# Down projections inside the MLP loops: one 128-row weight block by 1024 columns per unit, summed over a whole turn in four PSUM banks

## The chip, the cores and the metric

The kernel runs on one core of a Trainium2 chip. The metric is the device time of one execution in microseconds, as the median of several runs. Three runs of the kernel before gave 2069.18, 2069.45 and 2069.55 us.

## The reference, cut to what matters

Two layers of an encoder act on x, which has 256 rows of 2048 float32 values. Each layer adds the output of an attention stage and then that of an MLP with 8192 hidden columns. The change touches only the MLP's second product.

```python
for l in range(DEPTH):                      # DEPTH = 2
    ...                                     # attention stage, x = x + mixed @ w_out[l]
    h2 = rmsnorm(x, norm2_g[l])             # x: (256, 2048)
    x = x + jnp.square(jax.nn.relu(h2 @ w_up[l])) @ w_down[l]
    # w_up[l]: (2048, 8192), w_down[l]: (8192, 2048)
```

## The kernel before

**Units.** All large products are cut into units of weights. A unit is a tile of 128 partitions by 2 by 512 float32 values (512 KB) in one of the eight slots of `raw_ring`. In the MLP a unit of w_up holds two row blocks of 128 rows by 512 columns, and so does a unit of w_down. SyncE loads it (line 389), up to eight units ahead. ScalarE (`split_hi`, line 715) rounds it to `w_hi`, and VectorE (`split_lo`, line 894) subtracts to get the rest, `w_lo`. The activations are held as two such halves too. Both `w_hi` and `w_lo` have four slots (`AHEAD` = 4), taken in turn, so that unit s + 4 goes where unit s was. `split_hi` of unit s + 4 therefore waits in `unit_done` until TensorE has finished unit s, and `split_lo` of it waits in `hi_ready` for `split_hi`.

**Order.** Each engine runs a program written out in steps s, one per unit. In step s TensorE multiplies unit s, while ScalarE and VectorE first split unit s + 4 and then do the other work of the step. A layer has its attention steps, then 32 up units, then three turns (`LOOPS`) of 32 down units and 32 up units, then 32 down units. Each turn consumes the hidden columns (2048 of them, `ht`, hi and lo) of the up units before it.

**Down units before** (`rows_unit`, lines 482 to 504). A turn has eight chunks `c` of four units `k`. A chunk is 512 columns of x, summed over 1024 of the hidden columns; the sums of the two row halves of x (`r` = 0, 1) fill two PSUM banks. A unit is eight matmuls with `w_hi` (line 496, two row blocks, two halves of x, two halves of `ht`) and four with `w_lo` (line 500). Chunks take the bank pairs 4, 5 and 2, 3 in turn, and a chunk waits in `evicted` for the chunk before last. After a chunk's last unit VectorE adds both banks, scaled by `rstd`, to x (line 1164), in the step's program behind `split_lo(pl, s + AHEAD)` (line 1146).

**Up units** (`up_unit`, lines 506 to 521). A chunk of eight units fills four banks, 0 to 3 or 4 to 7 in turn (`up_banks`), by 8 matmuls of 512 columns (line 516) and 8 of 256 (line 519) in each unit. The first chunk of a turn's up units takes banks 4 to 7.

Of the kernel before, what the change touches and what calls it, by code (L numbers as in the profile page):

```python
# [24 lines left out]
ALU = mybir.AluOpType  # L25
# [3 lines left out]
P = 128  # L29
D = 2048  # L30
# [36 lines left out]

CHUNKS = NPROJ + 4 + 48  # L70
EVICTIONS = [(CHUNKS - 1) // 2, CHUNKS // 2]
LOOP_EVICTIONS = 6


SUMMED_UNITS = list(range(55, 83, 2))
# [85 lines left out]
def vector_splits(n):  # L161

    return n - sum(u < n for u in SUMMED_UNITS)
# [7 lines left out]
def encoder(nc, x_in, norm1_g, w_in, a_qnorm_g, a_knorm_g, a_rel_bias, b_qnorm_g, b_knorm_g, b_sinks, c_qnorm_g,  # L171
            c_knorm_g, c_lambda_q1, c_lambda_k1, c_lambda_q2, c_lambda_k2, c_subln_g, w_out, norm2_g, w_up, w_down,
            consts, out):
    with ExitStack() as ctx:
# [3 lines left out]
        def sem(name):  # L178
            return ctx.enter_context(nc.semaphore(name))
# [110 lines left out]
        mid_loaded = sem("mid_loaded")  # L290
        stored = sem("stored")
        row0_done, row0_out = sem("row0_done"), sem("row0_out")

        H_CHUNKS = 16

# [23 lines left out]
        def mlp_steps(first, kinds):  # L319


            s, n = first, {UP0: 13, LOOP0: 17, DOWN3: 17 + 36}[first]
            for kind in kinds:
                if kind == "up":
                    for q in range(4):
                        for k in range(UPC):
                            yield s, "up", q // 2, q, k, n
                            s += 1
                        n += 1
                else:  # L330
                    for c in range(8):
                        for k in range(4):
                            yield s, "down", c // 4, c, k, n
                            s += 1
                        n += 1

        def layer_steps(eng, l, do_mix, do_mlp):

            pl = Place(l)
            for s in range(UP0):  # L340
                do_mix(pl, s)
            for st in mlp_steps(UP0, ["up"]):
                do_mlp(pl, *st)
            for i in range(LOOPS):
                for st in mlp_steps(LOOP0, ["down", "up"]):
                    do_mlp(Place(l, i), *st)
            for st in mlp_steps(DOWN3, ["down"]):
                do_mlp(pl, *st)
# [11 lines left out]
        def late_chunk(s, part, c, k, lag):  # L360

            if part == "up":
                if k == lag and c > 0:
                    return c - 1, (c - 1) + (0 if s < LOOP0 else 4)
                return None
            if c == 0 and k == lag:

                return 3, 3 if s < DOWN3 else 3 + 4 * LOOPS
            return None

        def used(pl, s):
# [11 lines left out]
        def _(sp):  # L383
            def load(pl, u, w, width, offset, cols):
                if u - RAWS in SUMMED_UNITS:
                    sp.wait_ge(*lo_sum_of(pl, u - RAWS))
                else:
                    sp.wait_ge(split_done, pl.at(VECTOR_SPLITS, vector_splits(u - RAWS + 1) + RAWS, LOOP_UNITS))
                sp.dma_start(raw_ring[:, u % RAWS, :, 0:cols],
                             bass.AP(w.tensor, offset, [[width, P], [P * width, 2], [1, cols]])).then_inc(raw_loaded[u % RAWS], 16)  # L390
# [31 lines left out]
            def load_up(pl, u, c, k):  # L422

                i = 0 if pl.i is None else pl.i
                col = (c + (0 if u < LOOP0 else 4)) * CW + i * (4 * CW)
                load(pl, u, w_up, D_FF, pl.l * (D * D_FF) + k * 2 * P * D_FF + col, CW)

            def load_down(pl, u, c, k, past=False):
                i = 0 if pl.i is None else pl.i
                row = (c // 4 + (2 * LOOPS if past else 0)) * (D_FF // 8) + k * 2 * P  # L430
                load(pl, u, w_down, D, pl.l * (D_FF * D) + i * (2 * (D_FF // 8) * D) + (row * D + (c % 4) * CW), CW)

            def mlp(pl, s, part, buf, c, k, n):

                u = s + FIRST_LOADS
                if part == "up":
                    n = c * UPC + k + FIRST_LOADS
                    if n < 4 * UPC:
                        load_up(pl, u, n // UPC, n % UPC)
                    elif s < LOOP0:  # L440
                        load_down(pl, u, 0, n - 4 * UPC)
                    else:
                        load_down(pl, u, 8, n - 4 * UPC)
                else:
                    n = c * 4 + k + FIRST_LOADS
                    if n < 32:
                        load_down(pl, u, n // 4, n % 4, s >= DOWN3)
                    elif s < DOWN3:
                        load_up(pl, u, 0, n - 32)
                    elif pl.l < DEPTH - 1:  # L450
                        load_proj(pl, u, pl.l + 1)

# [22 lines left out]
        def _(pe):  # L475
# [30 lines left out]
            def up_unit(pl, u, k, chunk):  # L506

                slot, p, bank = u % AHEAD, chunk % 2, up_banks(chunk)
                if k == 0:
                    pe.wait_ge(evicted[p], pl.evictions(chunk))  # L510
                pe.wait_ge(hi_ready, pl.unit(u + 1))
                tiles = [(2 * k + j, f, slot, j) for j in range(2) for f in range(4)]
                for kt, f, w, j in tiles:
                    both = xt_both[:, kt, :, :].rearrange("p h q -> p (h q)")

                    pe.matmul(bank[:, f, :], w_hi[:, w, j, f * P:(f + 1) * P], both, start=kt == 0, stop=False, skip_group_check=True)  # L516
                unit_is_split(pl, u)
                for kt, f, w, j in tiles:
                    mm = pe.matmul(bank[:, f, 0:SEQ], w_lo[:, w, j, f * P:(f + 1) * P], xt[0][:, kt, :], start=False,  # L519
                                   stop=kt == KT - 1, skip_group_check=True)  # L520
                mm.then_inc(unit_done, 1)

            def warm(n):

# [144 lines left out]
            def mlp(pl, s, part, buf, c, k, n):  # L669
                if part == "up":  # L670
                    if s < LOOP0 and c == 0:
                        pe.wait_ge(panel_done, pl.at(PANELS, PANELS_BEFORE + FIRST_X2 + k + 1))
                    if s == UP0:
                        pe.wait_ge(maxed, pl.at(JOBS, JOBS + 1))
                        pe.wait_ge(pt_copied, pl.at(FILLS, FILLS + 1))
                    if s == UP0 + UPC:
                        pe.wait_ge(pv_copied, pl.at(MIXES, MIXES + 1))
                        pe.wait_ge(t_free, pl.at(T_USES, T_BEFORE + T_NUMBER[OUT_LAST[3] + 4] + 1))
                    up_unit(pl, s, k, n)
                else:  # L680
                    if k == 0 and c % 4 == 0:

                        done = (4 if s >= DOWN3 else 0) + 2 * (buf + 1) + (8 if s >= DOWN3 else 0)
                        pe.wait_ge(h_done, pl.at(H_CHUNKS, done, 4))
                    rows_unit(pl, s, ht, (8 * buf + 2 * k, 8 * buf + 2 * k + 1), n, k == 0, k == 3, CW)
                if s in T_USE and used(pl, s):
                    use_t(pl, s)
# [195 lines left out]
        def _(dve):  # L883
# [257 lines left out]
            def mlp(pl, s, part, buf, c, k, n):  # L1141
# [4 lines left out]
                    split_lo(pl, s + AHEAD)  # L1146
                if s == UP0 + 2:
                    row_norm(pl, 1)
                if part == "down" and k == 3:
                    p = n % 2  # L1150
                    if c == 0:
                        dve.wait_ge(rstd_ready, pl.at(2, 2))
                    final = pl.l == DEPTH - 1 and s == UNITS - 1
                    if not final:
                        dve.wait_ge(unit_done, pl.unit(s + 1 + AHEAD))
                    dve.wait_ge(evicted[p], pl.evictions(n))
                    for r in range(RT):
                        v = x[:, r, (c % 4) * CW:(c % 4 + 1) * CW]
                        if final and r == 0:
                            dve.wait_ge(row0_done, 1)  # L1160
                        if final and r == 1:
                            last.then_inc(row0_out, 1)
                            dve.wait_ge(unit_done, pl.unit(s + 1 + AHEAD))
                        last = dve.scalar_tensor_tensor(v, acc[:, 2 * p + r, :], rstd[:, 1, r:r + 1], v, ALU.mult, ALU.add)  # L1164
                    last.then_inc(evicted[p], 1)
# [6 lines left out]
                late = late_chunk(s, part, c, k, 0)  # L1172
                if late is not None:
                    q, count = late
                    m = n - 1
                    dve.wait_ge(evicted[m % 2], pl.evictions(m) + 1)
                    dve.scalar_tensor_tensor(mlp_t[q % 2][:, :], mlp_t[q % 2][:, :], 0.0, mlp_t[q % 2][:, :], ALU.max,  # L1177
                                             ALU.mult).then_inc(relu2, 1)
# [202 lines left out]
```

## Time and profile before

| | |
|---|---|
| median of three runs | 2069.45 us (2069.18 to 2069.55) |
| span of the profiled execution, first to last instruction | 2067.1 us |
| own time of the profiled execution | not listed separately; the runs' median is 2.35 us above its span |
| TensorE busy | 2061.8 us |
| VectorE busy | 1267.3 us |
| ScalarE busy | 990.7 us |
| DMA, mean | 192 GB/s |

The profile records one execution. PE is TensorE's matmuls and PEld its weight loads, DVE is VectorE, ACT is ScalarE, POOL is GpSimd and SP is SyncE; a "q" behind a name is the engine's instruction queue. Matmul records overlap their neighbours, so the spacing of two starts, and not the duration of one, tells what a matmul costs in a row. Lines with x and a number are several instructions merged, and their duration is that of the group from its first start to its last end.

### The profile page before, as it was taken

How to read it: one execution, taken by the hardware profiler on the slowest of the kernel's cores; microseconds unless marked ns; L12 is line 12 of the kernel's file. 1: busy time of each engine (PE TensorE's matmuls, PEld its weight loads, DVE VectorE, ACT ScalarE, POOL GpSimd, SP SyncE). 2: the span in 40 equal slices, each digit the busy share in tenths (PEclk: the TensorE clock that was granted, in tenths of full speed). 3: DMA queues.
4: the chain of work that ended last, by engine and by line, in shares of the span. 5: the costliest groups of instructions: out<-in, count | busy, mean ns of one | idle time of the engine just before them, and what ended most of it. 6: DMA issues, size and time to landing. Idle time of an engine off the chain costs nothing.

```text
span 2067.1 us, 26774 instructions
## 1 busy us (share of the span) xinstructions
PE 2061.8 (100%) x10762; PEld 1733.5 (84%) x10762; DVE 1267.3 (61%) x1646; ACT 990.7 (48%) x1328; POOL 191.7 (9%) x196
## 2 busy tenths in 40 slices
PE   9999999999999999999999999999999999999999
PEld 7887788888888888888888877888888888888887
DVE  7767566655565556556677775665655655665664
ACT  6557644443443444344455586444434434434442
POOL 6253100000000000001023531000000000000000
PEclk9999999999999999999999999999999999999999
DMA  9477866666666666666665689666666666666663
GB/s 301 136 229 194 225 184 184 191 191 192 189 192 194 187 190 193 193 185 193 183 178 148 205 203 242 176 183 190 192 192 190 192 194 187 191 193 192 186 193 122
DMA packets 207451, 396.64 MB, mean 192 GB/s; under 512 B 13674, under 2 KB 22352, under 8 KB 207328
## 3 DMA queue, kind: packets, MB, share of 16 engines
q1 hardware_dynamic: 202640, 379.52, 61.9%
q0 software_dynamic: 4512, 15.33, 4.0%
q8 instruction: 85, 1.39, 0.3%
q14 instruction: 38, 0.31, 0.0%
q10 hardware_dynamic: 176, 0.09, 0.0%
HBM read 377.95 MB, written 2.12 MB: 184 GB/s over the span
## 4 chain that ended last, share of the span: by engine, by line
PE 99%; DMA 0%; SPq 0%; DVE 0%; issue 0%
PE psum L496 40%; PE psum L516 23%; PE psum L500 20%; PE psum L519 12%; PE psum L531 1%; PE psum L603 1%; PE psum L582 0%; PE psum L628 0%; PE psum L590 0%; PE psum L588 0%; DMA x<-in_x_dram 0%; PE psum L638 0%; PE psum L619 0%; PE psum L620 0%; PE psum L618 0%; PE psum L640 0%
## 5 line engine op out<-in xcount | busy, mean ns | idle before, releaser
L894 DVE TENSOR_TENSOR w_lo<-raw_ring,w_hi 128x1024 fp32r<-128x1024 f32 (+1 forms) x692 | 850.9, 1231 | 680.8 <-ACT w_hi L715 679.4
L715 ACT CAST w_hi<-raw_ring 128x1024 fp32r<-128x1024 f32 (+1 forms) x720 | 749.7, 1042 | 995.3 <-PE psum L500 604.1
L516 PE MATMUL psum<-xt,w_hi 128*128 128x512 f32 x2048 | 512.9, 392 | 0.0
L496 PE MATMUL psum<-w_hi,ht_hi 128*128 128x512 f32 x1280 | 501.8, 392 | 0.0
L496 PE MATMUL psum<-w_hi,ht_lo 128*128 128x512 f32 x1280 | 498.6, 390 | 0.0
L516 PEld LDWEIGHTS psum<-xt,w_hi 128*128 128x128 f32 x2048 | 368.8, 189 | 66.3
L500 PE MATMUL psum<-w_lo,ht_hi 128*128 128x512 f32 x1280 | 342.5, 389 | 0.0
L519 PEld LDWEIGHTS psum<-xt,w_lo 128*128 128x128 f32 x2048 | 279.4, 190 | 19.9
L519 PE MATMUL psum<-xt,w_lo 128*128 128x256 f32 x2048 | 285.6, 282 | 0.0
L500 PEld LDWEIGHTS psum<-w_lo,ht_hi 128*128 128x128 f32 x1280 | 240.3, 188 | 50.3
L496 PEld LDWEIGHTS psum<-w_hi,ht_hi 128*128 128x128 f32 x1280 | 240.4, 188 | 49.6 <-issue 1.0
L496 PE MATMUL psum<-w_hi,xt 128*128 128x512 f32 (+1 forms) x1152 | 281.5, 386 | 0.0
L496 PEld LDWEIGHTS psum<-w_hi,ht_lo 128*128 128x128 f32 x1280 | 240.5, 188 | 48.8
L496 PEld LDWEIGHTS psum<-w_hi,xt 128*128 128x128 f32 x1152 | 202.4, 188 | 40.9 <-issue 2.7
L500 PE MATMUL psum<-w_lo,xt 128*128 128x512 f32 (+1 forms) x576 | 147.8, 378 | 0.0
L500 PEld LDWEIGHTS psum<-w_lo,xt 128*128 128x128 f32 x576 | 104.8, 188 | 21.1 <-DMA w_lo<-raw_ring 0.3
L1164 DVE SCALAR_TENSOR_TENSOR x<-psum,rstd,x 128x512 f32<-128x512 f32 x128 | 89.9, 743 | 6.4 <-PE psum L500 6.4
L1278 POOL TENSOR_TENSOR rope_c<-const,gains 128x64 f32<-128x64 f32 x16 | 9.6, 597 | 706.9 <-DVE head_sq L1177 701.1
L1028 DVE COPY probs_t<-psum 128x256 f32<-128x256 f32 (+1 forms) x56 | 26.8, 479 | 39.8 <-PE psum L603 39.8
L730 ACT CAST xt<-panel 128x512 fp32r<-128x512 f32 x32 | 19.9, 620 | 53.1 <-DVE panel L919 52.9
L1286 POOL TENSOR_TENSOR small<-small 128x16 f32<-128x16 f32 (+2 forms) x16 | 40.8, 2549 | 1.3
L1340 POOL DMA_DIRECT2D w_lo<-raw_ring x28 | 24.6, 897 | 130.1 <-ACT w_lo L717 130.1
(144 smaller groups left out, 968.2 us busy)
## 6 DMA issues: line engine op xcount, KB each, us to landing
raw_ring<-in_w_up_dram SPq DMA_DIRECT2D x256, 512.0 KB, 3.7
raw_ring<-in_w_down_dram SPq DMA_DIRECT2D x256, 512.0 KB, 3.7
raw_ring<-in_w_in_dram SPq DMA_DIRECT2D x128, 512.0 KB, 4.7
raw_ring<-in_w_out_dram SPq DMA_DIRECT2D x64, 512.0 KB, 4.8
w_lo<-raw_ring POOLq DMA_DIRECT2D x28, 512.0 KB, 5.8
raw_ring<-in_w_in_dram SPq DMA_DIRECT2D x16, 256.0 KB, 2.8
x<-in_x_dram SPq DMA_DIRECT2D x8, 256.0 KB, 7.5
out_dram<-x SPq DMA_DIRECT2D x3, 512.0 KB, 2.7
```

The source lines that it names most:

```text
L496: pe.matmul(bank[r][:, 0:cols], t[:, kt, r * P:(r + 1) * P], w_hi[:, slot, j, 0:cols], start=first and j == 0 and n == 0, stop=False, skip ...
L500: mm = pe.matmul(bank[r][:, 0:cols], src[0][:, kt, r * P:(r + 1) * P], w_lo[:, slot, j, 0:cols], start=False, stop=last and j == 1, skip_g ...
L516: pe.matmul(bank[:, f, :], w_hi[:, w, j, f * P:(f + 1) * P], both, start=kt == 0, stop=False, skip_group_check=True)
L519: mm = pe.matmul(bank[:, f, 0:SEQ], w_lo[:, w, j, f * P:(f + 1) * P], xt[0][:, kt, :], start=False, stop=kt == KT - 1, skip_group_check=True)
L531: mm = pe.transpose(bank[:, n * P:(n + 1) * P], b, ident)
L603: mm = pe.transpose(ps_p[:, n * P:(n + 1) * P], probs[:, j % 4, n * P:(n + 1) * P], ident)
L715: act.copy(w_hi[:, u % AHEAD, :, 0:cols], raw_ring[:, u % RAWS, :, 0:cols]).then_inc(hi_ready, 1)
L894: dve.tensor_tensor(w_lo[:, u % AHEAD, :, 0:cols], raw_ring[:, u % RAWS, :, 0:cols], w_hi[:, u % AHEAD, :, 0:cols].bitcast(F32), ALU.subtr ...
L1028: dve.tensor_copy(probs_t[:, f % 3, cols], ps_p[:, cols]).then_inc(pt_copied, 1)
L1164: last = dve.scalar_tensor_tensor(v, acc[:, 2 * p + r, :], rstd[:, 1, r:r + 1], v, ALU.mult, ALU.add)
L1286: return pool.tensor_tensor(dst, v, minus_half[:, 0:n], ALU.pow)
L1340: pool.dma_start(w_lo[:, u % AHEAD, :, :], raw_ring[:, u % RAWS, :, :], accum_op=ALU.add).then_inc(lo_sum_of(pl, u)[0], 16)
```

## The change

In the three turns of both layers, the 32 down units are now `pair` steps. A unit is one row block of 128 rows by 1024 columns, loaded in rows of 4 KB (before: two row blocks by 512 columns, in rows of 2 KB). Sixteen units `m` run over all 16 row blocks of the turn, for the left 1024 columns of x (`d` = 0) and then for the right ones (`d` = 1). The sums for two halves of x and two halves of the columns lie in banks 4 to 7, and are added to x after m = 15, one bank at a time. Both values of `d` use the same four banks, and so does the first chunk of up units that follows. TensorE therefore waits in `pair_out` for bank n before it starts the new sum there. In the last unit of a sum, TensorE finishes one bank after the other and signals `pair_done` for the first three. The 32 down units at the end of a layer stay as they were.

The diff, cut to its core:

```diff
-CHUNKS = NPROJ + 4 + 48
+CHUNKS = NPROJ + 4 + 4 + 4 * LOOPS + 8
 EVICTIONS = [(CHUNKS - 1) // 2, CHUNKS // 2]
-LOOP_EVICTIONS = 6
+LOOP_EVICTIONS = 2
+
+
+PAIR_UNITS = 32
+BLOCKS = 2 * UPC
+PAIR_OUTS = 4
...
+                if kind == "pair":
+                    for d in range(2):
+                        for m in range(BLOCKS):
+                            yield s, "pair", None, d, m, None
+                            s += 1
...
+        def pair_at(pl, u):
+
+            w = u - LOOP0 + LOOP_UNITS * (pl.i or 0)
+            if 0 <= w < LOOPS * LOOP_UNITS and w % LOOP_UNITS < PAIR_UNITS:
+                return w // LOOP_UNITS, w % PAIR_UNITS // BLOCKS, w % BLOCKS
...
+            def load_pair(pl, u, turn, d, m):
+
+                sp.wait_ge(split_done, pl.at(VECTOR_SPLITS, vector_splits(u - RAWS + 1) + RAWS, LOOP_UNITS))
+                sp.dma_start(raw_ring[:, u % RAWS, :, :].rearrange("p j n -> p (j n)"),
+                             bass.AP(w_down.tensor, pl.l * (D_FF * D) + (turn * D + m * P) * D + d * 2 * CW,
+                                     [[D, P], [1, 2 * CW]])).then_inc(raw_loaded[u % RAWS], 16)
...
+                    if kt == 0 and pl.i is not None and chunk == 17:
+                        pe.wait_ge(pair_out, pl.at(2 * LOOPS * PAIR_OUTS, PAIR_OUTS + f + 1, 2 * PAIR_OUTS))
...
+            def pair_step(pl, s, d, m):
+
+                outs = pl.at(2 * LOOPS * PAIR_OUTS, d * PAIR_OUTS, 2 * PAIR_OUTS)
+                if d == 0 and m in (0, UPC):
+                    pe.wait_ge(h_done, pl.at(H_CHUNKS, 2 + 2 * (m // UPC), 4))
+                if d == 0 and m == 0:
+                    pe.wait_ge(evicted[1], pl.evictions(17))
+                pe.wait_ge(hi_ready, pl.unit(s + 1))
+                if m == BLOCKS - 1:
+                    unit_is_split(pl, s)
+                for n in range(4):
+                    r, h = n // 2, n % 2
+                    bank = psum[:, 4 + n, :]
+                    if d == 1 and m == 0:
+                        pe.wait_ge(pair_out, outs - PAIR_OUTS + 1 + n)
+                    for j, t in enumerate(ht):
+                        pe.matmul(bank, t[:, m, r * P:(r + 1) * P], w_hi[:, s % AHEAD, h, :], start=m == 0 and j == 0,
+                                  stop=False, skip_group_check=True)
+                    if m == BLOCKS - 1:
+                        mm = pe.matmul(bank, ht[0][:, m, r * P:(r + 1) * P], w_lo[:, s % AHEAD, h, :], start=False, stop=True,
+                                       skip_group_check=True)
+                        mm.then_inc(pair_done if n < 3 else unit_done, 1)
+                if m < BLOCKS - 1:
+                    unit_is_split(pl, s)
+                    for n in range(4):
+                        r, h = n // 2, n % 2
+                        mm = pe.matmul(psum[:, 4 + n, :], ht[0][:, m, r * P:(r + 1) * P], w_lo[:, s % AHEAD, h, :], start=False,
+                                       stop=True, skip_group_check=True)
+                    mm.then_inc(unit_done, 1)
...
                     split_lo(pl, s + AHEAD)
                 if s == UP0 + 2:
                     row_norm(pl, 1)
+                if part == "pair" and k == BLOCKS - 1:
+                    if pl.i == 0 and c == 0:
+                        dve.wait_ge(rstd_ready, pl.at(2, 2))
+                    for g in range(4):
+                        r, h = g // 2, g % 2
+                        if g < 3:
+                            dve.wait_ge(pair_done, pl.at(2 * LOOPS * 3, 3 * c + g + 1, 6))
+                        else:
+                            dve.wait_ge(unit_done, pl.unit(s + 1 + AHEAD))
+                        v = x[:, r, (2 * c + h) * CW:(2 * c + h + 1) * CW]
+                        dve.scalar_tensor_tensor(v, psum[:, 4 + g, :], rstd[:, 1, r:r + 1], v, ALU.mult, ALU.add).then_inc(pair_out, 1)
```

## Rows read from the trace of the kernel before

**Rows 1.** The page's span and busy times of all engines.

```profile
span 2067.1 us, 26774 instructions
...
PE 2061.8 (100%) x10762; PEld 1733.5 (84%) x10762; DVE 1267.3 (61%) x1646; ACT 990.7 (48%) x1328; POOL 191.7 (9%) x196
```

**Rows 2.** The page's chain that ended last, by engine and by line.

```profile
PE 99%; DMA 0%; SPq 0%; DVE 0%; issue 0%
PE psum L496 40%; PE psum L516 23%; PE psum L500 20%; PE psum L519 12%; PE psum L531 1%; PE psum L603 1%; PE psum L582 0%; PE psum L628 0%; PE psum L590 0%; PE psum L588 0%; DMA x<-in_x_dram 0%; PE psum L638 0%; PE psum L619 0%; PE psum L620 0%; PE psum L618 0%; PE psum L640 0%
```

**Rows 3.** Busy times, granted clock (PEclk), DMA share and GB/s, a stretch of the first layer's loops.

```profile
core 0: us, PE busy (x) PEld busy (x) DVE busy (x) ACT busy (x) POOL busy (x), PEclk, DMA share, GB/s
...
545.00:700.00 155.00, 155.00 (x775) 131.92 (x775) 89.45 (x82) 64.84 (x63) 0.00 (x0) 1.00 0.66 191
```

**Rows 4.** TensorE in order of time, around a down unit's end.

```profile
start us, us, engine line op out<-in xcount [idle before <-releaser]
429.60 0.62 PE L500 MATMUL psum<-w_lo,ht_hi 128*128 128x512 f32 x2
430.05 0.39 PE L496 MATMUL psum<-w_hi,ht_hi 128*128 128x512 f32 x1
430.27 0.39 PE L496 MATMUL psum<-w_hi,ht_lo 128*128 128x512 f32 x1
...
431.86 1.07 PE L500 MATMUL psum<-w_lo,ht_hi 128*128 128x512 f32 x4
432.77 0.39 PE L496 MATMUL psum<-w_hi,ht_hi 128*128 128x512 f32 x1
```

**Rows 5.** TensorE in order of time, up units.

```profile
520.15 2.00 PE L516 MATMUL psum<-xt,w_hi 128*128 128x512 f32 x8
521.99 1.11 PE L519 MATMUL psum<-xt,w_lo 128*128 128x256 f32 x8
522.94 2.00 PE L516 MATMUL psum<-xt,w_hi 128*128 128x512 f32 x8
```

**Rows 6.** ScalarE in order of time, the down unit's end.

```profile
430.30 1.05 ACT L715 CAST w_hi<-raw_ring 128x1024 fp32r<-128x1024 f32 x1 [1.67 <-PE psum L500]
```

**Rows 7.** VectorE in order of time, the down unit's end.

```profile
431.38 1.23 DVE L894 TENSOR_TENSOR w_lo<-raw_ring,w_hi 128x1024 fp32r<-128x1024 f32 x1 [0.36 <-ACT w_hi L715]
432.53 1.40 DVE L1164 SCALAR_TENSOR_TENSOR x<-psum,rstd,x 128x512 f32<-128x512 f32 x2
434.11 1.23 DVE L894 TENSOR_TENSOR w_lo<-raw_ring,w_hi 128x1024 fp32r<-128x1024 f32 x1 [0.18 <-ACT w_hi L715]
```

**Rows 8.** The page's DMA issues of the down weights: count, KB each, us to landing.

```profile
raw_ring<-in_w_down_dram SPq DMA_DIRECT2D x256, 512.0 KB, 3.7
```

**Rows 9.** The page's costliest groups, additions onto x: count, busy us, mean ns, idle before.

```profile
L1164 DVE SCALAR_TENSOR_TENSOR x<-psum,rstd,x 128x512 f32<-128x512 f32 x128 | 89.9, 743 | 6.4 <-PE psum L500 6.4
```

**Rows 10.** VectorE, 8 to 10 us, a tile TensorE waits for.

```profile
8.35 1.22 DVE L894 TENSOR_TENSOR w_lo<-raw_ring,w_hi 128x1024 fp32r<-128x1024 f32 x1
```

**Rows 11.** TensorE's weight loads, 8 to 10 us.

```profile
9.62 0.53 PEld L500 LDWEIGHTS psum<-w_lo,xt 128*128 128x128 f32 x3 [0.23 <-DVE w_lo L894]
```

**Rows 12.** TensorE in order of time, the kernel's start.

```profile
1.14 1.65 PE L692 MATMUL psum<-panel 128*128 128x128 f32 x6 [1.14 <-DVE panel L1225]
...
2.96 1.54 PE L526 MATMUL psum<-const 128*128 128x128 f32 x6
4.29 0.91 PE L531 MATMUL psum<-const,x 128*128 128x128 f32 x4
5.03 1.25 PE L526 MATMUL psum<-const 128*128 128x128 f32 x10
7.05 0.66 PE L531 MATMUL psum<-const,x 128*128 128x128 f32 x4 [0.76 <-DMA x<-in_x_dram]
...
9.67 1.14 PE L500 MATMUL psum<-w_lo,xt 128*128 128x512 f32 x4
```

**Rows 13.** The warming transposes' line: count, duration in ns min/median/max.

```profile
L526 PE MATMUL psum<-const x18: 272/273/474, 3.0 to 7.7; 128*128 128x128 f32 x18
```

**Rows 14.** Busy times and granted clock (PEclk), two stretches of the start.

```profile
3.00:4.00 1.00, 1.00 (x6) 1.00 (x6) 0.19 (x1) 0.00 (x0) 0.00 (x0) 1.00 0.73 200
...
5.00:6.00 1.00, 1.00 (x11) 1.00 (x10) 0.69 (x1) 0.00 (x0) 0.00 (x0) 1.00 0.93 299
```

More of the change, by code:

```diff
@@ L292, in encoder @@
         row0_done, row0_out = sem("row0_done"), sem("row0_out")
+        pair_done, pair_out = sem("pair_done"), sem("pair_out")
         H_CHUNKS = 16
@@ L319, in mlp_steps @@
         def mlp_steps(first, kinds):
-            s, n = first, {UP0: 13, LOOP0: 17, DOWN3: 17 + 36}[first]
+            s, n = first, {UP0: 13, LOOP0: 17, DOWN3: 17 + 4 * LOOPS}[first]
             for kind in kinds:
-                if kind == "up":
+                if kind == "pair":
[3 more added lines that the diff above has]
+                            s += 1
+                elif kind == "up":
                     for q in range(4):
@@ L344, in layer_steps @@
             for i in range(LOOPS):
-                for st in mlp_steps(LOOP0, ["down", "up"]):
+                for st in mlp_steps(LOOP0, ["pair", "up"]):
                     do_mlp(Place(l, i), *st)
@@ L368, in late_chunk @@
                 return 3, 3 if s < DOWN3 else 3 + 4 * LOOPS
+            return None
+        def pair_at(pl, u):
+            w = u - LOOP0 + LOOP_UNITS * (pl.i or 0)
+            if 0 <= w < LOOPS * LOOP_UNITS and w % LOOP_UNITS < PAIR_UNITS:
+                return w // LOOP_UNITS, w % PAIR_UNITS // BLOCKS, w % BLOCKS
             return None
@@ L426, in load_up, with load_down @@
                 load(pl, u, w_up, D_FF, pl.l * (D * D_FF) + k * 2 * P * D_FF + col, CW)
[L428 to L431, printed above, removed]
+            def load_down(pl, u, c, k):
+                row = (c // 4 + 2 * LOOPS) * (D_FF // 8) + k * 2 * P
+                load(pl, u, w_down, D, pl.l * (D_FF * D) + (row * D + (c % 4) * CW), CW)
+            def load_pair(pl, u, turn, d, m):
[3 more added lines that the diff above has]
+                                     [[D, P], [1, 2 * CW]])).then_inc(raw_loaded[u % RAWS], 16)
             def mlp(pl, s, part, buf, c, k, n):
                 u = s + FIRST_LOADS
-                if part == "up":
+                if pair_at(pl, u) is not None:
+                    load_pair(pl, u, *pair_at(pl, u))
+                elif part == "pair":
+                    load_up(pl, u, 0, u - LOOP0 - PAIR_UNITS)
+                elif part == "up":
                     n = c * UPC + k + FIRST_LOADS
@@ L439, in mlp @@
                         load_up(pl, u, n // UPC, n % UPC)
-                    elif s < LOOP0:
+                    else:
                         load_down(pl, u, 0, n - 4 * UPC)
-                    else:
-                        load_down(pl, u, 8, n - 4 * UPC)
                 else:
@@ L446, in mlp @@
                     if n < 32:
-                        load_down(pl, u, n // 4, n % 4, s >= DOWN3)
-                    elif s < DOWN3:
-                        load_up(pl, u, 0, n - 32)
+                        load_down(pl, u, n // 4, n % 4)
                     elif pl.l < DEPTH - 1:
@@ L679, in mlp @@
                     up_unit(pl, s, k, n)
+                elif part == "pair":
+                    pair_step(pl, s, c, k)
                 else:
                     if k == 0 and c % 4 == 0:
-                        done = (4 if s >= DOWN3 else 0) + 2 * (buf + 1) + (8 if s >= DOWN3 else 0)
-                        pe.wait_ge(h_done, pl.at(H_CHUNKS, done, 4))
+                        pe.wait_ge(h_done, pl.at(H_CHUNKS, 4 * LOOPS + 2 * (buf + 1)))
                     rows_unit(pl, s, ht, (8 * buf + 2 * k, 8 * buf + 2 * k + 1), n, k == 0, k == 3, CW)
@@ L1148, in mlp @@
                     row_norm(pl, 1)
+                if part == "pair" and k == BLOCKS - 1:
[5 more added lines that the diff above has]
+                            dve.wait_ge(pair_done, pl.at(2 * LOOPS * 3, 3 * c + g + 1, 6))
+                        else:
+                            dve.wait_ge(unit_done, pl.unit(s + 1 + AHEAD))
+                        v = x[:, r, (2 * c + h) * CW:(2 * c + h + 1) * CW]
+                        dve.scalar_tensor_tensor(v, psum[:, 4 + g, :], rstd[:, 1, r:r + 1], v, ALU.mult, ALU.add).then_inc(pair_out, 1)
                 if part == "down" and k == 3:
@@ L1174, in mlp @@
                     q, count = late
-                    m = n - 1
+                    m = 16 if part == "pair" else n - 1
                     dve.wait_ge(evicted[m % 2], pl.evictions(m) + 1)
```

## The prediction

> **What bounds the kernel now.** I read the page's busy times first: TensorE is busy for 2061.8 of 2067.1 us, while VectorE stands at 1267.3 and ScalarE at 990.7 [rows 1]. The reader should see that an edit can only shorten this kernel by making TensorE's own stream shorter, since TensorE idles for 5.3 us in all. The chain that ended last says the same: 99% of it is TensorE, and all of it that matters is matmul lines [rows 2]. In a stretch of the loops TensorE is busy for all of 155.00 us, at a granted clock of 1.00, and the DMA engines are busy for 0.66 of it [rows 3]. So no wait ends last in the loops: there is no waiting left to take away there, only waiting to add.
>
> Then I looked at the cost of one unit. The spacing of matmul starts counts. In a down unit the eight with w_hi start at 430.05 and the four with w_lo at 431.86, so the spacing is 1.81 / 8 = 0.227 us. The next unit starts at 432.77, so a unit takes 2.72 us [rows 4]. In an up unit eight matmuls last 2.00 us from first start to last end; with 0.39 for the last one the spacing is 1.61 / 7 = 0.23 us, and the unit takes 522.94 - 520.15 = 2.79 us [rows 5].
>
> Last I looked at what happens when a unit ends, because the change makes TensorE wait there. The unit that ends at 430.22 (two matmuls from 429.60, 0.62 us long [rows 4]) frees its slot of w_hi. ScalarE's rounding of the unit four ahead starts at 430.30 and takes 1.05 us [rows 6]. Only then can VectorE's subtraction for that unit start, at 431.38, and behind it in VectorE's program stands the addition onto x, at 432.53 [rows 7]. So the addition starts 2.48 us after TensorE has begun the next unit (432.53 - 430.05). In the kernel before nobody waits for it: the next chunk uses the other pair of banks, and its own banks are wanted again only four units, or 10.9 us, later.
>
> **The change part by part.**
>
> *Matmuls.* A pair unit has 4 x 2 matmuls with w_hi and 4 with w_lo, all of 512 columns: 12, as before, from the same kinds of operand. There are 6 turns x 32 = 192 such units. Only the bank order differs. I cost this at nothing, at 0.227 us each. Bounds: the nearest rows of another loop, the up units', have 0.230 us [rows 5], which would add 2304 x 0.003 = 7 us at most. A gain isn't excluded but small, since 1 ns each is 2.3 us and the rows of two quite different orders (0.227 and 0.230) differ by 3 ns.
>
> *Loads.* 512 KB per unit as before, in half as many rows of twice the length. A load lands in 3.7 us [rows 8], and is issued about eight units (21.8 us) ahead of its use, so it could take several times as long before anyone noticed. It costs nothing and brings nothing; if that cover were gone, TensorE would wait for DMA, which it does nowhere in the loops now. SyncE's wait for each load is the same wait in split_done, so its queue isn't delayed.
>
> *Additions onto x.* Before, a turn had 8 chunks x 2 of them, now 2 x 4. That is 6 x 8 = 48 fewer, at 0.743 us each [rows 9] some 36 us of VectorE's time. VectorE has 1267 us of work in 2067 [rows 1] and TensorE waits for it nowhere in the loops, so the saving is worth nothing.
>
> *The wait in h_done for the second half of the hidden columns* comes at m = 8 instead of unit 16. The last of these tiles is made in steps 0 to 2 of the turn by both programs, five units earlier than needed. Nothing.
>
> *The new waits in pair_out.* This is what I think decides. Before m = 15 of d = 0 the four banks can't be added, and d = 1 starts in the same banks at once. The signals pair_done are given early, in the last unit itself, but VectorE can't use them: in step m = 15 its program first has split_lo of the unit four ahead, which waits for split_hi, which waits in unit_done for the end of this very unit. So the first addition starts no earlier than now, 2.48 us after TensorE would have started d = 1. TensorE's queue is in order, so everything behind that wait stands as well.
>
> Take the rows of the boundary at 430.05 as a template. The first addition runs from 432.53 to 432.53 + 0.743 = 433.27 [rows 7, 9]. From a VectorE result to TensorE's next weight load 0.05 us pass (8.35 + 1.22 = 9.57 against 9.62) [rows 10, 11], and the matmul starts 0.05 us after the load (9.67) [rows 12]. So TensorE starts at 433.37 instead of 430.05: 3.32 us late. It then needs a bank each 2 x 0.227 = 0.45 us, but two additions take 1.40 us together, so one follows another by 1.40 - 0.74 = 0.66 us [rows 7]. The additions set the pace for three more banks: bank four is started at 433.37 + 3 x 0.66 = 435.35, and its pair ends its turn at 435.80. Undisturbed it would have been 430.05 + 8 x 0.227 = 431.86. The loss between d = 0 and d = 1 is 3.94 us.
>
> After d = 1 the up units take the same banks, and there each bank gets only one matmul before the next is wanted. The fourth starts at 435.35 as well and is through at 435.58, against 430.05 + 4 x 0.23 = 430.97: a loss of 4.61 us. What is late next? Three more units are already split, and VectorE is through with its four additions about 5.0 us after the old unit's end (432.53 - 430.22 = 2.31, then 3 x 0.66 + 0.74), before TensorE ends the delayed unit, 2.72 + 3.94 = 6.7 us after it was due to start. So nothing is handed on, and the loss of each stall stands alone.
>
> Into d = 0 of a turn there is no such wait: the up chunk before it lies in banks 0 to 3, and the one before that was emptied eight units ago.
>
> There are 6 turns, with one of each: 6 x (3.94 + 4.61) = 51.3 us. Bounds from the rows: if only the first bank's wait counted, 12 x 3.32 = 40 us; if each addition, now with a signal of its own, ran its full 0.743 us and no more overlapped its neighbour, 12 x 3 x 0.09 = 3 us more, so 54 us, and with the first bound on the matmuls 61 us.
>
> **The sum.** 2067.1 + 51.3 = 2118.4 us of span. The runs' median lies 2.35 us above the profile's span, so 2120.8 us.
>
> **A rule on the clock.** At the kernel's start six transposes take 1.54 us and ten take 1.25 us a little later [rows 12]; with 0.47 and 0.27 for the last of each (the longest and the median record of that line [rows 13]) the spacings are 0.21 and 0.11 us, a factor of two, as between 1.2 and 2.4 GHz, although the granted clock reads 1.00 in both stretches [rows 14]. The slow pace was over by the group at 5.03, and a gap of 0.76 us at 7.05 did not bring it back. This case has no longer gap, so it can't say what one of 3.3 us does. The Trainium skill ("TensorE: Matmul & The Clock Gate", "Why this matters for your kernels") says that idle gaps of TensorE between bursts can put it back to 1.2 GHz; it speaks against this change, as the stalls above are such gaps. No run here shows it yet. By it the sum would be that of the second rival below; without it the 51 us stand.
>
> **The rivals.**
>
> 1. *The evictions slip under the last unit, and nothing is lost.* The code in TensorE's last unit finishes banks 0.68 us apart (3 x 0.227), an addition every 0.66 us would keep up, and bank n would be free long before d = 1 asks. This needs VectorE to reach the additions before unit m = 15 ends. Against it stands the order of [rows 4, 6, 7]: rounding, subtraction, addition, each behind the unit's end, and the new additions stand at the same place of the program. If it held, the time would be 2069.4, and any nanosecond that the longer rows or fewer additions take off the matmuls' spacing would come on top: at 2 ns, 4.6 us, it would be 2065 and faster. That is the point from which this rival decides.
>
> 2. *The stalls also lower the clock.* If each stall is followed by a slow stretch as long as the start's, about 3.6 us (from the first matmul at 1.14 to somewhere in the group at 4.29, which still takes 0.91 us where the same four take 0.66 later [rows 12]), the pairs after a d = 0 sum take 0.91 instead of 0.66 us per bank: 3.63 against 2.43 us, 1.2 more. Into the up units a matmul of 0.46 stays under the 0.66 at first, then the rest of the stretch is lost by half: about 0.8. That makes 6 x 2.0 = 12 us, so 2133. If the rest of the unit runs slowly too, it is about 2.1 for each stall, 25 us, so 2146. I take the middle, 2140. What speaks for it is the stall of 3.3 us followed by 2 us at partial load; against it, that the largest gap of this trace, 0.76 us, changed nothing.
>
> 3. *Only the first wait counts.* The additions come closer together than 0.66 us, or TensorE's next bank is always there. Then it's 40 us: 2109. The spacing of 0.66 was measured on the same instruction, so I give it little.
>
> **How the numbers follow.** The stall by VectorE's order as costed: 0.70. With the clock: 0.19. Only the first wait: 0.07. No stall: 0.04, of which 0.01 with a gain. Less than 0.2% (4 us) is what a measurement of this kernel can't tell from no change, so faster has 0.01, the same 0.03, slower 0.96. The likeliest case alone reaches from 2115 to 2131 us (its bounds on the matmuls and the additions). The range takes in the third rival and the second's upper price: 2109 to 2146.
>
> **What would show it.** The trace of the changed kernel should have, at 12 places, TensorE idle for about 3.2 us with VectorE's addition to x as what ends the wait; four additions in a row, 0.66 us apart; one long idle and three short ones in front of the first matmuls of d = 1 and of the up units; 80 additions in place of 128 [rows 9]; a matmul spacing of 0.227 us in the pair units; DMA at the same GB/s outside the stalls. With 12 stalls of another length, the product 12 x length gives the error. If the first addition started before the last unit's end, or TensorE's waits named something else, the main step would be wrong; if matmuls after the stalls were spaced by 0.45 us, the clock rival would be right.

## The result, and the profile after

The changed kernel takes 2141.43 us (median of four runs, 2135.6 to 2142.1) against 2069.31 us before (now four runs): a ratio of 1.0342 (of the runs' means, like all ratios below), 95% interval 1.0327 to 1.0356. Three of the four runs lie at 2141.3 to 2142.1 us with a mean clock of 0.985 to 0.986, the fourth at 2135.6 us with 0.987, so the low clock does not cost the same in every run. The profiled execution took 2141.25 us with a span of 2139.4 us.

The page's head, and the chain that ended last by engine, against [rows 1, 2]:

```profile
span 2139.4 us, 26662 instructions
...
PE 2096.0 (98%) x10762; PEld 1751.9 (82%) x10762; DVE 1234.5 (58%) x1598; ACT 990.6 (46%) x1328; POOL 190.8 (9%) x196
...
PE 97%; DVE 1%; ACT 1%; DMA 1%; issue 0%; SPq 0%; ACTq 0%
```

TensorE has done the same 10762 matmuls. Its busy time grew by 34 us, to 2096.0, although no matmul was added, and the rest of the span grew by 38 us, to 43. So TensorE stands still for longer, and it also takes longer over the same work. The second part has two causes, as shown below: after a stall it works at the pace at which banks come free, and its clock is lower.

The waits of TensorE, from the view of who waited for whom (total us, times, longest):

```profile
PE psum L565 <- DVE x L1216: 19.2, 6, 3.2
PE psum L542 <- DVE x L1216: 19.2, 6, 3.2
```

All twelve stalls are there, six in front of d = 1 (line 565) and six in front of the up units (line 542), each behind an addition onto x (line 1216) and 3.2 us long.

TensorE in order of time around the first boundary between d = 0 and d = 1, against [rows 4]:

```profile
462.14 0.39 PE L568 MATMUL psum<-w_lo,ht_hi 128*128 128x512 f32 x1
465.73 0.47 PE L565 MATMUL psum<-w_hi,ht_hi 128*128 128x512 f32 x1 [3.20 <-DVE x L1216]
466.03 0.40 PE L565 MATMUL psum<-w_hi,ht_lo 128*128 128x512 f32 x1
466.30 0.50 PE L565 MATMUL psum<-w_hi,ht_hi 128*128 128x512 f32 x1
466.63 0.40 PE L565 MATMUL psum<-w_hi,ht_lo 128*128 128x512 f32 x1
466.95 0.50 PE L565 MATMUL psum<-w_hi,ht_hi 128*128 128x512 f32 x1
467.29 0.59 PE L565 MATMUL psum<-w_hi,ht_lo 128*128 128x512 f32 x1
467.68 0.73 PE L565 MATMUL psum<-w_hi,ht_hi 128*128 128x512 f32 x1
468.20 0.63 PE L565 MATMUL psum<-w_hi,ht_lo 128*128 128x512 f32 x1
468.63 1.91 PE L575 MATMUL psum<-w_lo,ht_hi 128*128 128x512 f32 x4
470.34 0.58 PE L565 MATMUL psum<-w_hi,ht_hi 128*128 128x512 f32 x1
```

The spacing in the last unit of d = 0 is 0.227 us, as before. The first matmul of d = 1 was due at 462.14 + 0.23 = 462.36 and starts at 465.73, 3.37 us late. Then the matmuls come in pairs 0.57 and 0.65 us apart, at 465.73, 466.30 and 466.95, as the banks are freed. But from 467.29 on they are 0.4 to 0.5 us apart, and the four with w_lo at 468.63 take 1.91 us in place of 1.07. The unit after d = 1's first starts at 470.34. It was due at 462.36 + 2.72 = 465.08, so this stall costs 5.26 us.

VectorE in the same stretch, against [rows 7]:

```profile
463.69 1.23 DVE L951 TENSOR_TENSOR w_lo<-raw_ring,w_hi 128x1024 fp32r<-128x1024 f32 x1 [1.49 <-ACT w_hi L772]
464.84 2.72 DVE L1216 SCALAR_TENSOR_TENSOR x<-psum,rstd,x 128x512 f32<-128x512 f32 x4
```

The subtraction, and then four additions in a row: (2.72 - 0.74) / 3 = 0.66 us apart.

The same around the first boundary from d = 1 to the up units, against [rows 5]:

```profile
511.15 0.39 PE L568 MATMUL psum<-w_lo,ht_hi 128*128 128x512 f32 x1
514.74 4.38 PE L542 MATMUL psum<-xt,w_hi 128*128 128x512 f32 x8 [3.20 <-DVE x L1216]
518.92 1.91 PE L545 MATMUL psum<-xt,w_lo 128*128 128x256 f32 x8
520.63 2.62 PE L542 MATMUL psum<-xt,w_hi 128*128 128x512 f32 x8
523.09 1.11 PE L545 MATMUL psum<-xt,w_lo 128*128 128x256 f32 x8
524.03 2.00 PE L542 MATMUL psum<-xt,w_hi 128*128 128x512 f32 x8
```

Eight matmuls that took 2.00 us take 4.38, and then 2.62 in the next unit. The third up unit starts at 524.03. It was due at 511.38 + 2 x 2.79 = 516.96: 7.07 us lost.

Busy times and granted clock (PEclk) around these two boundaries, against [rows 3]:

```profile
core 0: us, PE busy (x) PEld busy (x) DVE busy (x) ACT busy (x) POOL busy (x), PEclk, DMA share, GB/s
460.00:474.00 14.00, 10.80 (x40) 7.77 (x39) 6.31 (x7) 3.49 (x4) 0.00 (x0) 0.88 0.38 115
508.00:524.00 16.00, 12.70 (x48) 9.76 (x47) 6.81 (x8) 3.14 (x3) 0.00 (x0) 0.79 0.40 119
```

The granted clock averages 0.88 over the first 14 us and 0.79 over the 16 us of the second. In the slow stretch the four matmuls with w_lo are (1.91 - 0.63) / 3 = 0.43 us apart, against 0.227: about the factor of two between the clock's two levels, 2.4 and 1.2 GHz. So it was at 1.2 GHz for 0.12 x 14 / 0.5 = 3.4 us and for 0.21 x 16 / 0.5 = 6.7 us. Before it fell TensorE had stood still for 3.2 us and then worked at the additions' pace; it rose again while matmuls ran without a gap. All twelve stalls are followed by a low stretch. Over 16 us from 4 us before TensorE resumes, the clock averages 0.89 at five of the six stalls after d = 0, and 0.79 at the sixth and at all six in front of the up units. The mean over the whole run is 0.985.

At the third boundary after d = 0 the first matmul behind the stall is already slow, with 0.76 us where the one at 465.73 took 0.47, so there the clock had fallen before TensorE resumed:

```profile
842.95 0.76 PE L565 MATMUL psum<-w_hi,ht_hi 128*128 128x512 f32 x1 [3.20 <-DVE x L1216]
```

### The profile page after: what moved, and what is told of

Its sections match the earlier page's. It is cut to its first block, busy times and chain, and to the rows that moved or that the text cites. A ratio compares the mean times of both kernels' runs of the same rounds, so it can differ in the third digit from the quotient of the medians.

```text
span 2139.4 us, 26662 instructions
## 1 busy us (share of the span) xinstructions
PE 2096.0 (98%) x10762; PEld 1751.9 (82%) x10762; DVE 1234.5 (58%) x1598; ACT 990.6 (46%) x1328; POOL 190.8 (9%) x196
## 2 busy tenths in 40 slices
DMA packets 182874, 396.63 MB, mean 185 GB/s; under 512 B 13674, under 2 KB 22352, under 8 KB 182752
## 4 chain that ended last, share of the span: by engine, by line
PE 97%; DVE 1%; ACT 1%; DMA 1%; issue 0%; SPq 0%; ACTq 0%
PE psum L542 23%; PE psum L520 22%; PE psum L565 17%; PE psum L545 12%; PE psum L524 11%; PE psum L575 8%; PE psum L587 1%; PE psum L659 1%; ACT w_hi L772 1%; DVE w_lo L951 1%; PE psum L568 1%; PE psum L638 0%; DVE x L1216 0%; DMA w_lo<-raw_ring 0%; PE psum L684 0%; PE psum L646 0%
## 5 line engine op out<-in xcount | busy, mean ns | idle before, releaser
L542 PE MATMUL psum<-xt,w_hi 128*128 128x512 f32 x2048 | 528.9, 400 | 19.4 <-DVE x L1216 19.2
L542 PEld LDWEIGHTS psum<-xt,w_hi 128*128 128x128 f32 x2048 | 375.4, 193 | 94.7 <-issue 21.6
L565 PE MATMUL psum<-w_hi,ht_hi 128*128 128x512 f32 x768 | 304.8, 397 | 19.2 <-DVE x L1216 19.2
L545 PEld LDWEIGHTS psum<-xt,w_lo 128*128 128x128 f32 x2048 | 284.5, 194 | 20.7
L545 PE MATMUL psum<-xt,w_lo 128*128 128x256 f32 x2048 | 290.3, 285 | 0.0
L520 PE MATMUL psum<-w_hi,ht_hi 128*128 128x512 f32 x512 | 203.0, 397 | 0.0
L575 PE MATMUL psum<-w_lo,ht_hi 128*128 128x512 f32 x720 | 194.6, 392 | 0.0
L575 PEld LDWEIGHTS psum<-w_lo,ht_hi 128*128 128x128 f32 x720 | 137.0, 190 | 29.1
L524 PE MATMUL psum<-w_lo,ht_hi 128*128 128x512 f32 x512 | 137.3, 389 | 0.0
L524 PEld LDWEIGHTS psum<-w_lo,ht_hi 128*128 128x128 f32 x512 | 96.1, 188 | 20.4
```

The lines of the kernel that those rows point to most:

```text
L520: pe.matmul(bank[r][:, 0:cols], t[:, kt, r * P:(r + 1) * P], w_hi[:, slot, j, 0:cols], start=first and j == 0 and n == 0, stop=False, skip ...
L524: mm = pe.matmul(bank[r][:, 0:cols], src[0][:, kt, r * P:(r + 1) * P], w_lo[:, slot, j, 0:cols], start=False, stop=last and j == 1, skip_g ...
L565: pe.matmul(bank, t[:, m, r * P:(r + 1) * P], w_hi[:, s % AHEAD, h, :], start=m == 0 and j == 0, stop=False, skip_group_check=True)
L575: mm = pe.matmul(psum[:, 4 + n, :], ht[0][:, m, r * P:(r + 1) * P], w_lo[:, s % AHEAD, h, :], start=False, stop=True, skip_group_check=True)
```

## The experiments

My theory was: the additions wait behind a subtraction that waits for the end of the unit, TensorE waits for the additions, and the stall lowers the clock. The rivals: the wait has another cause, the new units are dearer or cheaper by themselves, or the clock falls for another reason. The kernels of the first four runs share one chip and its runs of the kernel before (2069.78 us), the last two another (2069.01 us).

### Additions ahead of the subtraction

```diff
+                if part == "pair" and k == BLOCKS - 1:
...
                 if s < UNITS - 1 and more:
                     split_lo(pl, s + AHEAD)
-                if part == "pair" and k == BLOCKS - 1:
...
```

The block with the four additions is unchanged.

Expected: 

> In step m = 15 VectorE makes its four additions before, and not after, the subtraction for the unit four ahead. Theory (that subtraction holds the additions back until the unit's end): the additions start 2.48 us after the unit does, 0.24 us before it ends, so TensorE starts d = 1 about 0.6 us late, bank four 2.6 us after its due start less 1.4; loss 1.2 us into d = 1 and 1.9 us into the up units, 6 x 3.1 = 19 us, and no fall of the granted clock: 2088 us, clock 1.000. Rival (the wait is due to something else, such as the late end of the sums themselves or the four banks' reuse as such): TensorE still idles for about 3.2 us at 12 places, 2141 us.

Measured: 2089.07 us, ratio 1.0096 (1.0079 to 1.0113), clock 1.000. VectorE, then TensorE, in order of time around the first boundary of this kernel:

```profile
461.83 1.23 DVE L951 TENSOR_TENSOR w_lo<-raw_ring,w_hi 128x1024 fp32r<-128x1024 f32 x1 [1.49 <-ACT w_hi L772]
462.98 2.72 DVE L1212 SCALAR_TENSOR_TENSOR x<-psum,rstd,x 128x512 f32<-128x512 f32 x4
```

```profile
462.99 0.39 PE L568 MATMUL psum<-w_lo,ht_hi 128*128 128x512 f32 x1
463.87 0.47 PE L565 MATMUL psum<-w_hi,ht_hi 128*128 128x512 f32 x1 [0.49 <-DVE x L1212]
```

The additions start at 462.98, while the unit that began at 460.50 still runs, and TensorE resumes at 463.87 instead of 463.22. The next unit starts at 467.23, due 460.50 + 2 x 2.72 = 465.94: 1.29 us lost for 1.2 expected. TensorE at the boundary to the up units of this kernel:

```profile
507.80 0.39 PE L568 MATMUL psum<-w_lo,ht_hi 128*128 128x512 f32 x1
508.68 1.06 PE L542 MATMUL psum<-xt,w_hi 128*128 128x512 f32 x2 [0.49 <-DVE x L1212]
509.90 0.50 PE L542 MATMUL psum<-xt,w_hi 128*128 128x512 f32 x1 [0.16 <-DVE x L1212]
510.56 1.45 PE L542 MATMUL psum<-xt,w_hi 128*128 128x512 f32 x5 [0.16 <-DVE x L1212]
511.85 1.10 PE L545 MATMUL psum<-xt,w_lo 128*128 128x256 f32 x8
512.79 2.00 PE L542 MATMUL psum<-xt,w_hi 128*128 128x512 f32 x8
```

The second up unit starts at 512.79 against 507.80 + 0.23 + 2.79 = 510.82, so 1.97 us lost for 1.9. One moved block of VectorE's program is worth 52 us, the clock's share included. The rival is out: the order of VectorE's program makes the long stall. What remains is 6 x 3.26 = 19.6 us, and it too hangs on that order in part. The last matmul of the first bank's sum starts at 460.95 and has ended by 461.34, but VectorE's next piece of work is the subtraction of the step before, which waits for ScalarE until 461.83, and the additions follow it at 462.98. Had they run from 461.4 on, 0.66 us apart, the four banks would have been free from 462.1 to 464.1. My estimate is that d = 1, which needs them from 463.22 on and 0.45 us apart, would not have waited at all, and the up units, which need them 0.23 us apart, for some 0.3 us. No run tries it.

### The right half in other banks

```diff
-                    bank = psum[:, 4 + n, :]
-                    if d == 1 and m == 0:
-                        pe.wait_ge(pair_out, outs - PAIR_OUTS + 1 + n)
+                    bank = psum[:, 4 - 4 * d + n, :]
...
-                if d == 0 and m == 0:
-                    pe.wait_ge(evicted[1], pl.evictions(17))
+                if m == 0:
+                    pe.wait_ge(evicted[1 - d], pl.evictions(17 + d))
...
-                    if kt == 0 and pl.i is not None and chunk == 17:
-                        pe.wait_ge(pair_out, pl.at(2 * LOOPS * PAIR_OUTS, PAIR_OUTS + f + 1, 2 * PAIR_OUTS))
+                    if kt == 0 and pl.i is not None and chunk in (17, 18):
+                        pe.wait_ge(pair_out, pl.at(2 * LOOPS * PAIR_OUTS, PAIR_OUTS * (chunk - 17) + f + 1, 2 * PAIR_OUTS))
```

The matmuls with w_lo and VectorE's additions take the same banks. The last edit is in the up units.

Expected: 

> The right half's sums (d = 1) go to banks 0 to 3, the left half's stay in 4 to 7, all else as in the changed kernel. Theory (the whole loss is the reuse of the same four banks, and the matmuls, longer rows and fewer additions are worth nothing): no wait of TensorE in the loops, 0.227 us per matmul, granted clock 1.000, 2069 us within 3 us. Rival (part of the loss is the new units' own: bank order, 4 KB rows): a matmul spacing above 0.227 us, 2073 us or more. Rival (the new units are cheaper, hidden under the stalls): 2065 us or less.

Measured: 2069.19 us (ten runs, 2068.72 to 2070.84), ratio 0.9999 (0.999 to 1.0009), clock 1.000. TensorE in order of time over the same boundary, and then VectorE:

```profile
463.97 0.39 PE L566 MATMUL psum<-w_lo,ht_hi 128*128 128x512 f32 x1
464.19 0.39 PE L563 MATMUL psum<-w_hi,ht_hi 128*128 128x512 f32 x1
```

```profile
465.53 1.22 DVE L949 TENSOR_TENSOR w_lo<-raw_ring,w_hi 128x1024 fp32r<-128x1024 f32 x1 [1.49 <-ACT w_hi L770]
466.67 2.72 DVE L1214 SCALAR_TENSOR_TENSOR x<-psum,rstd,x 128x512 f32<-128x512 f32 x4
```

From the last matmul of d = 0 at 463.97 to the first of d = 1 at 464.19 there are 0.22 us, as inside a unit, although the additions come as late as ever, at 466.67. So the whole loss hangs on the reuse of banks. The units themselves, with rows of 4 KB, another order of banks and 48 fewer additions, are together worth nothing that can be measured: the rival of dearer units and that of cheaper ones are both out at 0.1%. That two of these parts cancel each other isn't excluded. (The additions are 48 + 32 = 80 in the changed kernel's profile, where [rows 9] has 128.)

### The stalls filled with matmuls

```diff
+            def fill(count):
+                for _ in range(count):
+                    pe.matmul(psum[:, 0, :], ht[0][:, BLOCKS - 1, 0:P], xt_both[:, 0, :, :].rearrange("p h q -> p (h q)"),
+                              start=True, stop=True, skip_group_check=True)
...
+                        fill(13)
```

The call stands ahead of the first wait in pair_out, in pair_step and in up_unit.

The results of these matmuls are used by nobody; the reference's computation is all there.

Expected: 

> The stalls stay, but TensorE fills each with 13 matmuls of 512 columns into the unused bank 0 (13 x 0.227 = 2.95 us of the 3.3 us), in front of its wait. Theory (the part beyond 51 us is the lower clock, and it falls because TensorE idles): more work, less time, since only the clock's share goes: granted clock 1.000, 2121 us. Rival (the clock falls for another cause, the load of the two us after the wait for instance, or the part beyond 51 us isn't the clock's): 2141 us or a little more.

Measured: 2122.04 us, ratio 1.0253 (1.0237 to 1.0268), clock 1.000. TensorE in order of time at the boundary to the up units:

```profile
511.01 3.11 PE L533 MATMUL psum<-xt,ht_hi 128*128 128x512 f32 x13
514.29 0.50 PE L550 MATMUL psum<-xt,w_hi 128*128 128x512 f32 x1 [0.17 <-DVE x L1226]
514.95 0.50 PE L550 MATMUL psum<-xt,w_hi 128*128 128x512 f32 x1 [0.16 <-DVE x L1226]
515.60 0.50 PE L550 MATMUL psum<-xt,w_hi 128*128 128x512 f32 x1 [0.16 <-DVE x L1226]
516.26 1.43 PE L550 MATMUL psum<-xt,w_hi 128*128 128x512 f32 x5 [0.16 <-DVE x L1226]
517.52 1.11 PE L553 MATMUL psum<-xt,w_lo 128*128 128x256 f32 x8
518.47 2.00 PE L550 MATMUL psum<-xt,w_hi 128*128 128x512 f32 x8
```

156 matmuls more, and 19 us less than the changed kernel. The stall's end and the pace of the banks are the same (514.29, 514.95, 515.60, 516.26, so 0.66 us apart), but now the next unit starts at 518.47 against 513.80 due: 4.67 us, where I had 4.61. At the first boundary of d = 1 the four matmuls with w_lo start at 469.28 against 463.45 + 1.81 = 465.26: 4.02 us for 3.94.

```profile
463.45 3.11 PE L533 MATMUL psum<-xt,ht_hi 128*128 128x512 f32 x13
...
469.28 1.09 PE L585 MATMUL psum<-w_lo,ht_hi 128*128 128x512 f32 x4
```

That makes 6 x 8.69 = 52.1 us, and 52.3 were measured. The rival that the work at partial load after the wait lowers the clock by itself is out: this work is unchanged, and the clock did not fall (1.00 around all twelve places). It also shows that the 19 us are the clock's. With them the 34 us that TensorE's busy time grew by are nearly accounted for: the additions' pace makes 6 x (4.02 - 3.20 + 4.67 - 3.20) = 13.7 us, and the clock 19.4.

### Only the first kind of stall filled

```diff
-                        fill(13)
+                        fill(0)
```

That is the call in up_unit; the one in pair_step keeps its 13.

Expected: 

> As the run with 13 matmuls in each stall, but only in the six between d = 0 and d = 1; the six in front of the up units stay empty. From the trace of the changed kernel the clock costs 5.3 - 3.9 = 1.3 to 1.4 us at one of the first kind and 7.1 - 4.6 = 2.5 us at one of the second. Theory (each stall pays its own clock): six of the first kind saved, 2133 us, and low clock only after the stalls in front of the up units. Rival (the clock's fall after one stall depends on the stall before it): another saving, 0 or 20 us.

Measured: 2131.9 us, ratio 1.0299 (1.0284 to 1.0315), clock 0.992. It saved 9.5 us where I had 8. The two boundaries of the first turn in this kernel:

```profile
460.00:474.00 14.00, 13.83 (x59) 10.38 (x58) 6.63 (x9) 4.20 (x4) 0.00 (x0) 1.00 0.46 136
508.00:524.00 16.00, 12.80 (x51) 9.93 (x50) 6.32 (x7) 4.18 (x4) 0.00 (x0) 0.79 0.43 105
```

The clock is 1.00 after the filled stall and 0.79 after the empty one, as in the changed kernel, and it is 1.00 at all six filled places. So each stall lowers the clock by itself, and the rival with 0 or 20 us is out. The length of the low stretch is less fixed: after two of the six empty stalls the clock averages 0.89 and not 0.79, where the changed kernel has 0.79 at all six. That can make the saving larger than the 8 us.

### Four matmuls, at the start or in the middle of the stall

```diff
-                        fill(13)
+                        pe.wait_ge(hi_ready, pl.unit(s + 4))
+                        fill(4)
```

Both calls are changed so (in up_unit the wait is for unit u + 4). The kernel with the four at the start lacks the wait.

Expected, at the start: 

> As the run with 13 matmuls in each of the 12 stalls, but with 4 (0.9 us) at each stall's start, so that about 2.3 us of idleness are left in one piece. With 13 it was 2122 us at clock 1.000, with none 2141 us at 0.985. If any work that breaks the stall keeps the clock: 2122 us, clock 1.000. If a gap of 2.3 us is still enough for it to fall, it falls at some or all of the stalls: 2127 to 2141 us, clock below 0.998.

Expected, in the middle: 

> The same 4 matmuls, but held back until ScalarE has rounded the unit four ahead, 1.1 us into the stall, so that two gaps of about 1.2 us are left instead of one of 2.3 us. If the longest single gap decides, the clock stays at 1.000 and the time is 2122 us, at or below that of the run with the 4 at the start. If the amount of work in the stall decides, both runs with 4 have the same clock and the same time.

Measured: 2134.9 us at the start (2129.21 to 2135.33; ratio 1.0312, 1.0297 to 1.0327) and 2132.4 us in the middle (2128.8 to 2135.8; ratio 1.03, 1.0283 to 1.0318), the clock 0.991 to 0.995 in both. Two boundaries of the kernel with the four in the middle, TensorE's idle pieces first:

```profile
463.38 0.39 PE L580 MATMUL psum<-w_lo,ht_hi 128*128 128x512 f32 x1
465.05 1.16 PE L533 MATMUL psum<-xt,ht_hi 128*128 128x512 f32 x4 [1.28 <-ACT w_hi L784]
466.88 0.50 PE L577 MATMUL psum<-w_hi,ht_hi 128*128 128x512 f32 x1 [0.67 <-DVE x L1228]
```

```profile
460.00:474.00 14.00, 12.05 (x50) 8.62 (x49) 7.04 (x8) 3.80 (x4) 0.00 (x0) 1.00 0.43 137
508.00:524.00 16.00, 13.58 (x56) 10.30 (x55) 6.59 (x8) 3.93 (x4) 0.00 (x0) 0.89 0.39 116
```

The idle time is now in pieces of 1.28 and 0.67 us, yet the clock still falls, at the second boundary (0.89) and not at the first (1.00). So a longest gap of 1.28 us does not keep the clock up, as the first case of my expectation had it. In the kernel with the four at the start the idle piece is 2.21 us long, and its clock falls at the same ten of the twelve places; it stays at 1.00 at the other two, the first boundary of each layer. The ranges of the two kernels overlap, and both sit at nearly the same clock. So where the four matmuls stand in the stall made no difference that shows. That fits the case that the amount of work in the stall decides. It doesn't show it: a gap between the 0.49 us of the kernel with the additions moved, which lowered nothing, and 1.28 us could also be enough by itself. Why the clock falls at some boundaries and not at others of the same shape, these runs don't tell.

## Why the prediction was right, and where it was off

*What bounds the kernel, and the free parts.* Right. With other banks, the matmuls, the loads, the additions saved and the earlier wait in h_done together give a ratio of 0.9999.

*The place of the stall.* Right, in all steps: twelve stalls, idle for 3.2 us each, an addition at their end, behind the subtraction. One of the signs isn't there as named: the view of waits has no three short idles behind each long one in the changed kernel, since the matmuls' records touch each other there; the waits show in the spacing of the pairs instead. Moving the additions ahead gave 2089.07 us; the same template gives 2088.

*The size of the stall without the clock.* 3.94 and 4.61 us were forecast, 4.02 and 4.67 were measured with the clock held: 52 us for 51.3. The bounds on the additions (0.74 in place of 0.66 us) and on the matmuls (0.230) did not come into play. The 2.35 us between span and time were 1.85 in the profiled execution of the changed kernel.

*The clock.* This is the step where the likeliest case, held at 0.70, was wrong: it put the clock at nothing, and so gave 2120.8 us. With the clock held, that time was met by 2122.04. In the changed kernel it costs 2141.4 - 2122.0 = 19.4 us. The second rival, at 0.19, named the mechanism and gave 2133 to 2146 with 2140 as its middle, and it is what happened. It priced a short low stretch at 1.2 and 0.8 us for the two kinds, and one that lasts a whole unit at 2.1 for each. Measured at the first boundaries are 5.26 - 4.02 = 1.2 us after d = 0 and 7.07 - 4.67 = 2.4 us in front of the up units, where the clock stayed low for twice as long. So the first kind was the short form and the second the long one, but for one long stretch after d = 0. All twelve at these prices would be 21.8 us, and the kernel as a whole paid 19.4. From one resumption of TensorE to the next, the changed kernel takes 0.94 to 2.07 us more than the filled one after a stall of the first kind (7.5 us for the six) and 1.70 to 2.40 after one of the second (12.8 us); the filled kernel reaches its first resumption 1.0 us later, which brings the sum to the spans' difference of 19.3. The time lies inside the stated range and outside the likeliest case's own 2115 to 2131, whose bounds left the clock out. That the rival's middle came within 2 us is luck in part: it averages a short stretch everywhere and a long one everywhere, and the kernel had some of each. The argument against this rival, that a gap of 0.76 us changed nothing, said little about one four times as long, and should not have held its chance at 0.19. The Trainium skill ("TensorE: Matmul & The Clock Gate", "Why this matters for your kernels") warns of such gaps between bursts. The trace agrees, with 0.985 for the mean clock.

*The other rivals.* The evictions do not slip under the last unit in the changed kernel. Once moved, the first starts 0.24 us before TensorE is due to start the next sum, so they hardly do there either. That only the first wait counts is out: the three later banks came 0.66 us apart. The fourth case, no stall, took other banks to come about.

## What to carry to other kernels

When a sum is to use the PSUM banks of the sum before it, ask where the evictions stand in the evicting engine's program, and not when their input is ready: a signal given early is worth nothing behind an instruction that waits for the end of the same unit. A second set of banks made the whole change free here; moving the evictions one place up brought 52 of 72 us back. Ask also whether the instruction ahead of the evictions waits for something late. The price of a matmul stream that stands still was here the 3.2 us of each stall, then the slower pace of the banks, and then a stretch at half clock worth 0.9 to 2.4 us, so a budget for such a stall takes all three. Filling the stalls with matmuls that nobody needs was 19 us faster than leaving them empty.

## What the runs showed of the hardware that I had not expected

Rows of 4 KB in place of 2 KB made the packets fewer by the 192 x 128 = 24,576 rows saved (from 207451 to 182874), but the busy share of the DMA engines hardly moved in a stretch without stalls: 0.66 [rows 3] and 0.65 in the kernel with other banks, at the same 191 GB/s:

```profile
545.00:700.00 155.00, 155.00 (x774) 131.87 (x773) 84.51 (x74) 64.76 (x63) 0.00 (x0) 1.00 0.65 191
```

And a pause of TensorE broken by 0.9 us of matmuls, into pieces of 1.28 and 0.67 us, still lowered the clock at ten of the twelve places of its profiled execution, while 2.95 us of matmuls in it kept it at 1.00 everywhere.
